# Gathering the u and the v row of an expert in two separate 4 KB transfers

## The reference, cut to what matters

```python
eidx = jnp.take_along_axis(cidx.reshape(...), pos, axis=-1)      # 16 experts for each token and head
g = jax.nn.softmax(best, axis=-1)
act = jax.nn.gelu(jnp.einsum('phkd,pd->phk', u_tab[eidx], xb))   # dot product of the token with row u
return jnp.einsum('phk,phkd->pd', (g * act).astype(xb.dtype), v_tab[eidx])  # weighted sum of the rows v
```

## Time and profile before

| what | value |
|---|---|
| median of three runs | 3174.97 us |
| the profiled execution: its time / its span | 3177.49 us / 3175.6 us |
| PE busy (matmuls) | 2640.8 us, 83% of the span |
| DVE busy | 2108.9 us, 66% |
| POOL busy | 1077.6 us, 34% |
| ACT busy | 679.6 us, 21% |
| moved by DMA | 930.65 MB, mean 293 GB/s |
| of it in the queue that POOL issues to | 822.20 MB, 63.2% of the 16 DMA engines' span |
| granted TensorE clock, mean | 0.956 |

### The profile page before, as it was taken

The page is one execution under the profiler, slowest core; times in us unless marked ns, Lnnn a source line. Parts: engine busy times, 40 slices in busy tenths (PEclk is TensorE's granted clock), DMA queues, the critical chain, the costliest instruction groups (busy, mean ns, idle before and its releaser), DMA issues. The chain is left out here.

```text
span 3175.6 us, 31187 instructions
## 1 busy us (share of the span) xinstructions
PE 2640.8 (83%) x9164; PEld 1303.7 (41%) x9164; DVE 2108.9 (66%) x4866; ACT 679.6 (21%) x1701; POOL 1077.6 (34%) x927
## 2 busy tenths in 40 slices
PE   4996999996899998787777787776987788887777
PEld 2441888883444443222322232223434444432222
DVE  2236334335567777888888888885575677778887
ACT  1025333331221211111111111112024222111111
POOL 0002233222144444444444444441000243344443
PEclk8997999998999999999999999998998899999999
DMA  5224000005499999999999999997422699999998
GB/s 203 80 100 195 1 1 1 1 1 216 168 400 400 398 405 396 421 421 417 416 421 421 420 413 421 420 420 296 169 69 93 255 419 420 420 419 411 421 421 333
DMA packets 137393, 930.65 MB, mean 293 GB/s; under 512 B 16954, under 2 KB 17978, under 8 KB 32330
## 3 DMA queue, kind: packets, MB, share of 16 engines
q0 software_dynamic: 113664, 822.20, 63.2%
q1 hardware_dynamic: 23636, 107.25, 8.9%
HBM read 928.26 MB, written 1.13 MB: 293 GB/s over the span
## 5 line engine op out<-in xcount | busy, mean ns | idle before, releaser
L1469 PE MATMUL psum<-ring,diag 128*128 128x512 f32 x3072 | 1495.7, 622 | 350.6 <-DVE diag L1588 348.7
L1347 POOL DMA_INDIRECT ring<-in_uv,experts x768 | 914.3, 1191 | 1283.8 <-PE psum L1469 1036.2
L1642 DVE CUSTOM_DVE_ANT_0 ring<-ring,hcur 128x1024 f32<-128x1024 f32 x768 | 941.6, 1226 | 303.6 <-DMA ring<-in_uv,experts 276.0
L1469 PEld LDWEIGHTS psum<-ring,diag 128*128 128x128 f32 x3072 | 558.0, 194 | 1200.1 <-DVE diag L1588 726.0
L1377 ACT ACTIVATE gel<-dots 128x1 f32<-128x1 f32 x768 | 148.6, 201 | 1419.3 <-DVE dots L1642 1418.0
L1588 DVE TENSOR_SCALAR diag<-ident,gel,wcur 128x128 f32<-128x128 f32 x768 | 257.6, 345 | 21.9 <-ACT gel L1377 21.9
L1059 DVE COPY_PREDICATED T<-level,psum 128x512 f32<-128x512 uint32 x80 | 58.6, 733 | 173.8 <-PE psum L824 173.8
L344 PE MATMUL psum<-zT,win_ring 128*128 128x512 f32 x368 | 161.4, 599 | 1.4 <-PEq L90 1.4
L1708 PE MATMUL psum<-wqkv_ring,zT 128*128 128x512 f32 x320 | 139.4, 598 | 1.4 <-PEq L90 1.4
L1448 PE MATMUL psum<-yT,w_q 128*128 128x512 f32 (+1 forms) x256 | 120.3, 572 | 2.6 <-issue 2.6
L344 PEld LDWEIGHTS psum<-zT,win_ring 128*128 128x128 f32 x368 | 70.2, 192 | 87.8 <-issue 87.8
(11 more groups left out here) (368 smaller groups left out, 2702.0 us busy)
## 6 DMA issues: line engine op xcount, KB each, us to landing
wmod<-in_w_mod SPq DMA_DIRECT2D x24, 1024.0 KB, 8.8
w_q<-in_w_q SPq DMA_DIRECT2D x36, 512.0 KB, 7.9
wmod<-in_w_mod POOLq DMA_DIRECT2D x16, 1024.0 KB, 5.5
ring<-in_uv,experts POOLq DMA_INDIRECT x768
wqkv_ring<-in_w_qkv SPq DMA_DIRECT2D x6, 2048.0 KB, 10.7
win_ring<-in_w_in SPq DMA_DIRECT2D x23, 512.0 KB, 3.6
wring<-in_w_mod SPq DMA_DIRECT2D x4, 2048.0 KB, 11.7
bc<-modulation_rows SPq DMA_DIRECT2D x14, 512.0 KB, 13.0
```

The source lines that it names most:

```text
L1347: nc.gpsimd.indirect_dma_start(ring[:, s % RING], None, uv, bass.IndirectOffsetOnAxis(ap=experts[:, n, j:j + 1], axis=0)).then_inc(row_in[ ...
L1469: m = nc.tensor.matmul(ps[:, c], diag[:, j % DIAGS], ring[:, j % RING, D + 512 * c:D + 512 * c + 512], start=(first and j == 0), stop=(las ...
L1642: nc.vector.tensor_tensor_reduce(u, u, hcur[:], 1.0, 0.0, ALU.mult, ALU.add, dots[:, j:j + 1]).then_inc(dot_done, 1)
```

## The change

The table `uv` is viewed as twice as many rows of 1024 floats (`halves`), so that expert e has its u row at 2e and its v row at 2e + 1. Each step is now gathered in two indirect DMAs of 128 rows of 4 KB. The u half is issued once the dot product of the slot's earlier step is made (`dot_done`), the v half once its matmul is done (`mm_done`), both by POOL and in this order. Each half has semaphores of its own; DVE still waits on `row_in`, now only for u, and PE gets a wait on `v_in` ahead of its matmuls. Routing writes two lists of row numbers (`experts`, `seconds`) in place of one, in three small instructions in place of one. The bytes moved and all arithmetic on the rows are the same.

```diff
-    uv = a[f"uv{layer}"]
+    halves = a[f"uv{layer}"].rearrange("e (x d) -> (e x) d", x=2)
...
+        seconds = ph.sb("seconds", [P, NU + 1, TOPK], U32)
+        chosen = ph.sb("chosen", [P, 1, TOPK])
...
+        v_in = ph.sems(*[f"v_in{i}" for i in range(RING)])
...
                         if s >= RING:
+                            pool.wait_ge(dot_done, s - RING + 1)
+                        nc.gpsimd.indirect_dma_start(
+                            ring[:, s % RING, 0:D], None, halves, bass.IndirectOffsetOnAxis(ap=experts[:, n, j:j + 1], axis=0)
+                        ).then_inc(row_in[s % RING], 16)
+                        if s >= RING:
                             pool.wait_ge(mm_done, DIAGS + s - RING + 1)
                         nc.gpsimd.indirect_dma_start(
-                            ring[:, s % RING], None, uv, bass.IndirectOffsetOnAxis(ap=experts[:, n, j:j + 1], axis=0)
-                        ).then_inc(row_in[s % RING], 16)
+                            ring[:, s % RING, D:2 * D], None, halves, bass.IndirectOffsetOnAxis(ap=seconds[:, n, j:j + 1], axis=0)
+                        ).then_inc(v_in[s % RING], 16)
...
                         pe.wait_ge(diag_done, n * TOPK + j + 1)
+                        pe.wait_ge(v_in[j % RING], (n * (TOPK // RING) + j // RING + 1) * 16)
...
-                        nc.vector.scalar_tensor_tensor(experts[:, bass.ds(n, 1)], sel[:, 0:1], float(NKEYS), sel[:, 1:2],
-                                                       ALU.mult, ALU.add).then_inc(routed, 1)
+                        step(nc.vector.scalar_tensor_tensor(chosen[:], sel[:, 0:1], float(NKEYS), sel[:, 1:2], ALU.mult, ALU.add))
+                        step(nc.vector.tensor_scalar(experts[:, bass.ds(n, 1)], chosen[:], 2.0, None, ALU.mult))
+                        nc.vector.tensor_scalar(seconds[:, bass.ds(n, 1)], chosen[:], 2.0, 1.0, ALU.mult, ALU.add).then_inc(routed, 1)
```

## The result

| | before | after |
|---|---|---|
| median of 4 runs each, side by side, us | 3176.51 | 3402.59 |
| lowest to highest, us | 3174.10 to 3178.42 | 3399.68 to 3413.47 |
| after / before, 95% interval | | 1.0722 [1.0708, 1.0737] |
| span of the profiled execution, us | 3175.6 | 3398.1 |

The changed kernel is slower by 226 us, 7.2%. Forecast: 3425 us, +247 us on the profiled execution.

What follows compares the result with a forecast made beforehand. The DMA was taken to set the beat before, POOL after the change. Layer 0 +174.5, layer 1 +83.5, start -3, tail -9, routing +0.7 made +247 us, forecast 3425 us, range for 8 in 10 3205 to 3640.

Steps and rivals of the forecast that it cites:

- POOL sets the beat, T = 2.92 us: Expert steps: POOL's two gathers, gaps and holds take 2.49 + 1.25/T, so each step takes 2.92 us; chance 0.70.
- The price is for the gather: POOL: a gather of 4 KB rows costs 0.94 us, as with 8 KB rows, since the row count of 128 stays.
- Rival C: A half gather is cheaper for POOL, under 1.25 us with gap and hold; DMA stays the bound, 3131 us; chance 0.08.
- The gap of 0.30 us: POOL: 0.30 us of idle time between two gathers, counted twice in each step.
- The hold: A gather starting during a DVE dot product is held until its end: mean excess 0.25 us at 2.5, scaling with 2.5/T.
- Sum of both layers: Longer beat over 503 intervals in layer 0 and 247 in layer 1: +174.5 and +83.5 us.
- Start: Start of each layer: one u gather issued before PE frees the first slot, -1.5 us each, -3 in all.
- Tail: End of each layer: nothing queued, last dot product about 4.7 us after its gather; -5.0 and -4.3 us, -9 in all.
- Routing: DVE: two more small instructions for each unit, 0.17 us each; first gather of each layer 0.35 us later, +0.7 us.
- 4 KB packets: DMA queue: 410 GB/s, 2.56 us for a step, hidden under 2.92; costs 0 to 0.06 us a step, under 30 us.
- Rival B: Gathers fall into the gaps between dot products; T about 2.65 us, +44 us, 3221 us; chance 0.14.
- Rival D: Phase locks badly, v always issued at the beginning of a dot product; T = 3.54 us, 3888 us; chance 0.06.

Runs made afterwards that it cites:

- experiment 1: Kernel before, with a second small gather of 128 rows of 256 B into a spare tile behind each 8 KB-row gather: 3461.4 us, 1.091.
- experiment 6: Kernel before plus a second gather of 16 rows of 256 B on 16 partitions behind each gather: 3452.8 us, 1.0888.
- experiment 8: Kernel before plus one POOL memset of 128x1536 floats behind each gather, no second gather: 3325.1 us, 1.0472.
- experiment 3: Changed kernel with the token row hcur in PSUM, so a dot product has one SBUF input; first token row copied later: 3466.0 us, 1.0924.
- Experiment 5: Kernel before with the token row hcur moved to PSUM: 3175.2 us, 1.0004.
- experiment 10: Changed kernel with the token row in PSUM and the u gather waiting for a dot product three steps later (LEAD = 5): 3221.1 us, 1.0148.
- experiment 11: Changed kernel with the token row in PSUM and a one-column POOL memset behind each gather: 3221.4 us, 1.0155.
- the second level of 3467.5 us: Changed kernel run again unaltered, on the second chip: 3467.5 us, 1.0907, against 3402.59 us at first.

## Why the prediction was right

**POOL sets the beat, T = 2.92 us.** Right; measured 2.886. The term was built of three parts, and each has been shown by itself. *The price is for the gather*: I had 0.94 us as one end and took it, with a plain 2 KB transfer as the other; the shortest gather of 4 KB rows takes 0.933 us and the shortest of 128 rows of 256 B 0.945 (experiment 1), and even 16 rows take 0.838 (experiment 6). Rival C fell with it. *The gap of 0.30 us* stays, and in experiment 8 it shrinks to 0.17 only where another kind of instruction stands in it. *The hold*: mean excess 1.128 - 0.94 = 0.19 us for one gather, forecast 0.25 x 2.5/2.92 = 0.21. Experiments 3, 5, 10 and 11 take the hold away by changing where one input lies (and with it when the first token row is copied; LEAD or a 0.12 us memset comes beside it in the last two), and the gathers of all four fall to 942 to 967 ns. The sentence of the Trainium skill on two SBUF inputs (SBUF — State Buffer, "Who interferes with whom") is thus borne out on the gathers, and its early probe by which such instructions didn't seem to stall DMA is not.

**Sum of both layers.** Forecast +174.5 and +83.5. Measured as in the forecast, from the first refill to the last gather: 503 x (2.886 - 2.573) = +157.4 in layer 0, and in layer 1 (3376.38 - 2676.55) - (3150.26 - 2512.44) = +62.0. One T for both layers was 17 us too much in layer 0 and 21 in layer 1, where the beat is 2.833. With the first gather 1.7 us later, the start, the tail and 0.3 us between the layers the parts add up to the 222.5 us between the spans. The sum's last step holds a slip: the +247 were added to an execution 2.5 us above the median, so that 3425 stands for +250 against 3174.97; by its own terms the forecast was 3422.

**Start.** Half wrong. In layer 0 one u gather was issued ahead (861.05, against v's first at 869.61), and no more until v had gone, as foreseen; from the first gather to the first refill it is 41.2 us in both kernels, so that the -1.5 is 0. In layer 1 it is 26.8 us instead of 17.0, where the forecast had -1.5: the ring takes 16 gathers to fill instead of 8, dot products begin meanwhile, and six u gathers in a row take 1.60 to 1.87 us, each starting within half a microsecond of a dot product's start (one at 2657.87 above). The forecast let the ring fill without a hold; these +9.8 us hide a part of the miss in T.

**Tail.** Forecast -5.0 and -4.3. Counted from the last u gather, as there, it is -3.8 and -2.3; counted from the last v gather, as the beats here are, -5.1 and -3.6. From last gather of u to last dot product it is 5.9 us (2319.96 to 2325.85) and 6.6 us, not 4.7: the landing, worked out from a plain transfer less half its bytes, was undersized, since the page of the profile has a u gather at 6.2 us from issue to landing even with half the bytes.

**Routing.** Two instructions were added; over the whole span the one that writes `experts` takes 322 ns in the mean, the one that writes `seconds` 175, where I had 167 for each. It is hidden in the beat. The first gather of layer 0 starts 1.7 us later (826.8 to 828.4); from the start of the product `hot` on L1582 to the last index instruction it is 2.76 us instead of 2.35, so 0.41 of it is this, and the rest arose ahead of it.

**4 KB packets.** I had 410 GB/s, 2.56 us, as the lower bound of T and counted it as hidden. Right on both: 408 and 409 GB/s in experiments 11 and 10, and not visible in the changed kernel. The price beside it was too low: 0 to 0.06 us for a step is up to 45 us in 750 steps, not less than 30, and experiment 11 shows 49 us for packets and second gather together.

**Rival B** fell: 806 of 1536 gathers start inside a dot product. **Rival D** fell as a whole, since the mean v gather is 1.17 us and the mean u gather 1.08; its phase, with u in place of v, shows only for some steps at the start of layer 1. **What I gave no chance to** is the second level of 3467.5 us. It lies inside the range, but through a mechanism that no rival named.

## What to carry to other kernels

Count the gathers of a step before their bytes: each indirect gather of 128 rows costs the issuing engine 0.94 us and a gap of 0.30 here, whatever the length of its rows, so splitting one costs little until their sum meets the DMA's beat and costs in full behind it. If that sum is near the beat, look at what runs on DVE beside it; one input of the dot product moved to PSUM was worth some 180 us between two runs without stalls, and nothing where POOL had idle time or where there were stalls. Before such a change, ask if a queue that is always full can gain anything at all from an earlier refill.

## What the runs showed of the hardware

**Stalls.** In seven kernels with two gathers for each step (those on the first two chips) DVE, PE, ACT and POOL stand still for up to 10 us at a time, not always together, with no wait that accounts for it; 69 to 395 us in sum on DVE from 830 to 3150 us. Experiment 5, with one gather for each step, has 0.2 us on one of the same chips, and the kernel before keeps its time on both. The first execution of the changed kernel and all four kernels on the third chip have none on DVE, two of these with two gathers for each step. In the 12 us ahead of a stall of 1.5 us or more about 9.0 gathers were issued (29 stalls in the changed kernel, 81 in experiment 3) against 8.0 in the mean of layer 0; but experiment 11 issues 9.0 all through layer 0 and has none, so dense issuing alone doesn't bring them. Nor does a low TensorE clock: from 1300 to 1600 us the granted clock is 0.91 in the mean in the changed kernel with stalls and 0.88 in experiment 8 without. What distinguishes the chips or the moments, whether the recording of the trace has a part in it, and the cause itself, stay open.

**POOL and DVE.** With a memset of 128x1536 on POOL the diagonal takes twice its mean time on DVE, 345 to 679 ns, while the dot product of two SBUF inputs keeps its 1.22 us.

**Price of a gather.** The shortest on POOL: 0.84 us for 16 rows of 256 B, 0.945 for 128 of them, 0.935 for 128 rows of 8 KB. A one-column memset behind a gather adds at most 0.01 us to its 1.24.
